# Splitting the norm before the first feed-forward: latents inside the projection, context inside the gated chunks

## The chip, the core and the metric

The kernel runs as one program on one core of a Trainium2 chip. The metric is the device time of one execution in microseconds (us), lower is better. Five engines work side by side, each on its own queue in the order in which its instructions stand: TensorE (PE, with its weight loads PEld), VectorE (DVE), ScalarE (ACT), GpSimd (POOL) and SyncE (SP, which issues the transfers). They wait for one another through semaphores.

## The reference, cut to what matters

Two transformer blocks of two layers each. The change lies in layer 0 of the first block, between the output projection of its mixer and its gated feed-forward. There are two token streams: 512 latents (`xl`) and 256 context tokens (`xc`), each of width 1024. Both take a residual, an RMS norm with modulation, and the feed-forward with a convolved gate of width 2816.

```python
def modulate(x, norm_w, shift, scale):
    return rms_norm(x, norm_w) * (1 + scale) + shift

def conv_ffn(h, w_up, conv_w, conv_b, w_down):
    up = h @ w_up
    gate, val = up[..., :D_FF], up[..., D_FF:]
    ...
    return (jax.nn.silu(gate_c) * val) @ w_down

    xl = xl + g1 * yl
    xl = xl + g2 * conv_ffn(modulate(xl, norm_ffn_w[l], sh2, sc2), ffn_w_up[l], ...)
    if with_ctx:
        xc = xc + cg1 * yc
        xc = xc + cg2 * conv_ffn(modulate(xc, norm_ffn_w[l], csh2, csc2), ffn_w_up[l], ...)
```

## The kernel before

Activations stand with features on the 128 partitions and tokens along the free axis, so width 1024 is eight tiles (`KT = 8`). Segment `s = 0` is the 512 latents, `s = 1` the 256 context tokens. A product in float32 is made of three rounded passes: a weight chunk is split into a high part (ACT, line 481, `split_hi`) and a low part (POOL, line 490, two halves, `split_lo`), the activation too, and PE adds high by high, low-activation by high and high by low weight (lines 888 to 890). Two slots hold weight chunks. The high part of chunk c+2 is written once PE has done with chunk c, and POOL and PE follow.

**The projection** (`wout0`, PE `project_both`) has eight chunks. Each is swept over the latents' eight tiles, then over the context's, and each sum goes to a PSUM bank of its own. DVE adds it to the residual X (line 3140), ACT squares it (590), DVE adds the squares up tile by tile in SA (601).

**The norm `n1`** has, for each segment, a mean on PE (line 637: the added squares and the last tile's square against a vector of ones), a root on ACT (660), a reciprocal on DVE (671, `invert`), and a spread on PE (683) that brings the factors back over the partitions into a bank. `means(pe, "n1")` does both means and then both spreads, behind the last chunk of the projection. Then each tile is made: DVE scales it out of the spread bank (691), ACT adds the shift into a high part (729) and, for odd tiles, writes the shifted whole (731), and the low part comes from DVE for even tiles (737) and from POOL for odd ones (744).

**The feed-forward** (`ffn`, stage `up0`) takes 44 weight chunks, four to a round: gate and value for two gated pairs, called c = 0 to 3 here. In the first round PE sweeps chunks 0 and 1 over the latents, then 0 and 1 over the context, and only chunk 0 waits for each tile of a segment (`h_there`). Chunk 2 follows, and from there the rest of `up0`. Before it makes the high part of chunk 2, ACT runs, in its own order, all shifts of both segments and then three Silu activations over condition vectors, which SP loads (line 1412, two into `arena` and one into the buffer of the squares, so only after the means have read it):

```python
                if l:
                    ...
                else:
                    late_silus((LATE_C, LATE_CC, LATE_C2), 3)
                with act.Fori(l, FT // 2 - 1) as i:
                    for c in range(2):
                        gate_pair(c, i)     # begins with split_hi(up, 2 * c + 2, 2 * i, (up, 2 * c, i))
```

POOL's order around the change is: low parts of chunks 0 and 1, odd tiles of the latents, odd tiles of the context, low parts of chunk 2 onward.

## Time and profile before

| what | value |
|---|---|
| time, median of 3 runs | 2271.38 us (2269.86 to 2274.02) |
| the profiled execution | 2269.67 us, of which its span is 2267.7 us |
| PE busy | 2211.0 us (98%), 13959 matmuls |
| DVE, ACT, POOL busy | 1177.3 (52%), 879.2 (39%), 932.8 us (41%) |
| granted PE clock, mean of the span | 0.995 |
| data moved | 245.40 MB, mean 108 GB/s |

Times in the views count from the start of the span. A bracket at a row's end is idle time just before the instruction, with what ended it. A row with "x3" stands for three instructions side by side, merged. The granted clock is 1.00 at 2.4 GHz and 0.50 at 1.2 GHz.

### The profile page before, as it was taken

The page shows a single profiled execution, that of the slowest core. Times are in us where ns is not written, and L with a number is a line of the kernel's source. Part 1 is how long each engine was busy: PE and PEld are TensorE (multiplying, and loading weights), DVE is VectorE, ACT ScalarE, POOL GpSimd, SP SyncE. Part 2 cuts the span into 40 slices and gives each one's busy share as a digit, 9 for nine tenths or more (in the row PEclk, how much of TensorE's full clock was granted, in tenths as well). Part 3 has the DMA queues.
Part 4 walks back from the last instruction along what each step waited for, and adds up shares of the span by engine and source line. Part 5 has one row for each costly group of instructions (what it writes and reads, how often), then busy time and mean ns, then how long its engine had stood idle before and what let it go on. Part 6 is the DMA issues. An engine that isn't in the chain of part 4 may idle for free.

```text
span 2267.7 us, 36911 instructions
## 1 busy us (share of the span) xinstructions
PE 2211.0 (98%) x13959; PEld 1900.5 (84%) x13959; DVE 1177.3 (52%) x1926; ACT 879.2 (39%) x1532; POOL 932.8 (41%) x767
## 2 busy tenths in 40 slices
PE   6999999999999999999999999999999999999998
PEld 4878979888888888889899988888888887788777
DVE  5785781657777763435244365553234115761273
ACT  5434353341111113325455442222444236742572
POOL 2435443343334443334353155555665441154323
PEclk9999999999999999999999999999999999999999
DMA  7242241125555541111211035553223332123212
GB/s 279 81 150 75 72 161 63 56 94 195 194 192 175 196 149 65 65 63 67 71 48 34 10 102 186 185 196 109 94 96 105 94 101 75 50 84 102 71 48 75
DMA packets 67720, 245.40 MB, mean 108 GB/s; under 512 B 7376, under 2 KB 11728, under 8 KB 66960
## 3 DMA queue, kind: packets, MB, share of 16 engines
q1 hardware_dynamic: 67360, 242.94, 31.3%
q8 instruction: 84, 1.38, 0.3%
q0 software_dynamic: 240, 0.79, 0.1%
q14 instruction: 36, 0.29, 0.0%
HBM read 240.81 MB, written 2.10 MB: 107 GB/s over the span
## 4 chain that ended last, share of the span: by engine, by line
PE 76%; issue 3%; DVE 2%; ACT 2%; POOL 1%; POOLq 0%; DVEq 0%; ACTq 0%
PE ps L888 14%; PE ps L889 14%; PE ps L890 14%; PE ps L1780 4%; PE ps L1783 4%; PE ps L1782 4%; PE ps L2010 2%; PE ps L1996 2%; PE ps L1948 1%; PE ps L925 1%; PE ps L926 1%; PE ps L927 1%; PE ps L637 1%; PE ps L2027 1%; POOL w_low L490 1%
## 5 line engine op out<-in xcount | busy, mean ns | idle before, releaser
L490 POOL TENSOR_TENSOR w_low<-ring,w_high 128x512 fp32r<-128x512 f32 (+2 forms) x534 | 746.0, 1418 | 1030.5 <-ACT w_high L481 1023.8
L481 ACT ACTIVATE w_high<-ring 128x1024 fp32r<-128x1024 f32 (+2 forms) x267 | 275.2, 1032 | 918.8 <-PE ps L890 623.7
L888 PE MATMUL ps<-h_high,w_high 128*128 128x512 f32 x1040 | 407.7, 392 | 4.4 <-DVE h_low L737 2.8
L889 PE MATMUL ps<-h_low,w_high 128*128 128x512 f32 x1040 | 405.9, 390 | 0.0
L890 PE MATMUL ps<-h_high,w_low 128*128 128x512 f32 x1040 | 405.4, 390 | 0.0
L888 PEld LDWEIGHTS ps<-h_high,w_high 128*128 128x128 f32 x1040 | 195.9, 188 | 47.9 <-issue 4.1
L890 PEld LDWEIGHTS ps<-h_high,w_low 128*128 128x128 f32 x1040 | 195.6, 188 | 41.4
L889 PEld LDWEIGHTS ps<-h_low,w_high 128*128 128x128 f32 x1040 | 195.9, 188 | 38.1
L3246 DVE TENSOR_TENSOR hidden<-arena,hidden 128x1536 fp32r<-128x1536 f32 (+1 forms) x42 | 87.2, 2076 | 193.3 <-ACT hidden L2363 193.3
L2913 DVE CUSTOM_DVE_ANT_0 const<-const,arena 128x1024 f32<-128x1024 f32 x96 | 154.9, 1629 | 56.5 <-DMA const<-late_w_dram 56.5
L1780 PE MATMUL ps<-hidden,w_high 128*128 128x512 f32 (+1 forms) x504 | 178.6, 354 | 0.0
L1782 PE MATMUL ps<-hidden,w_high 128*128 128x512 f32 (+1 forms) x504 | 178.5, 354 | 0.0
L1783 PE MATMUL ps<-hidden,w_low 128*128 128x512 f32 (+1 forms) x504 | 178.3, 354 | 0.0
L1783 PEld LDWEIGHTS ps<-hidden,w_low 128*128 128x128 f32 x504 | 95.2, 189 | 13.4
L890 PE MATMUL ps<-h_ctx_high,w_low 128*128 128x256 f32 x376 | 106.4, 283 | 0.0
L889 PE MATMUL ps<-h_ctx_low,w_high 128*128 128x256 f32 x376 | 106.4, 283 | 0.0
L1780 PEld LDWEIGHTS ps<-hidden,w_high 128*128 128x128 f32 x504 | 95.3, 189 | 13.2
L1782 PEld LDWEIGHTS ps<-hidden,w_high 128*128 128x128 f32 x504 | 95.3, 189 | 13.2
L888 PE MATMUL ps<-h_ctx_high,w_high 128*128 128x256 f32 x376 | 106.3, 283 | 0.0
L2592 ACT ACTIVATE arena<-arena 128x512 f32<-128x512 f32 (+2 forms) x128 | 81.0, 634 | 38.6 <-DVE arena L3430 38.3
L3169 DVE TENSOR_SCALAR arena<-ps,vecs 128x512 f32<-128x512 f32 x65 | 46.6, 717 | 65.9 <-PE ps L890 56.7
L889 PEld LDWEIGHTS ps<-h_ctx_low,w_high 128*128 128x128 f32 x376 | 72.0, 191 | 1.7
(553 smaller groups left out, 4747.8 us busy)
## 6 DMA issues: line engine op xcount, KB each, us to landing
const<-late_w_dram SPq DMA_DIRECT2D x112, 512.0 KB, 5.0
ring<-up_dram SPq DMA_DIRECT2D x88, 512.0 KB, 3.3
ring<-down_dram SPq DMA_DIRECT2D x44, 512.0 KB, 3.2
XB<-ada_dram SPq DMA_DIRECT2D x22, 768.0 KB, 5.4
ring<-winE_dram SPq DMA_DIRECT2D x32, 512.0 KB, 3.5
ring<-win_dram SPq DMA_DIRECT2D x20, 512.0 KB, 3.2
ring<-winC_dram SPq DMA_DIRECT2D x20, 512.0 KB, 3.5
arena<-ada_dram SPq DMA_DIRECT2D x10, 768.0 KB, 19.7
```

Source lines behind the costliest of these rows:

```text
L481: nc.scalar.activation(WH[p][:, 0:L], RAW[p][:, 0:L], ACT.Copy).then_inc(w_hi, 1)
L490: ins = nc.gpsimd.tensor_tensor(WL[p][:, to], RAW[p][:, to], WH[p][:, to].bitcast(F32), ALU.subtract)
L888: nc.tensor.matmul(bank[:, 0:n], wh[:, cols], hi, start=(k == 0), stop=False)
L889: nc.tensor.matmul(bank[:, 0:n], wh[:, cols], lo, start=False, stop=False)
L890: ins = nc.tensor.matmul(bank[:, 0:n], wl[:, cols], hi, start=False, stop=(k == kt - 1))
L1780: MM(to, wh[:, cols], hi, start=start and m % per == 0 and j == 0, stop=False, skip_group_check=True)
L1782: MM(to, wh[:, cols], lo, start=False, stop=False, skip_group_check=True)
L1783: ins = MM(to, wl[:, cols], hi, start=False, stop=stop and j == 1, skip_group_check=True)
L2592: A(at, at, ACT.Exp, scale=-1.0, bias=column(NM, kind, u, x), accum_out=column(LSUM, kind, u, x)).then_inc(e_p, 1)
L2913: nc.vector.tensor_tensor_reduce(LATE_W[t], LATE_W[t], vectors[x + t], 1.0, 0.0, ALU.mult, ALU.add, LATE_SUM[:, x + t:x + t + 1]).then_inc ...
L3169: TS(FA[:, c, a:a + n], bank[:, 0:n], cw[:, bass.ds(i * 2 + (FT + c), 1)], V(f"cb{l}")[:, bass.ds(i * 2 + c, 1)], ALU.mult, ALU.add).then_ ...
L3246: TT(lo, inner_pair(c, width, i), hi.bitcast(F32), ALU.subtract).then_inc(g_lo, 1)
```

## The change

The projection's last two chunks are swept in another order: chunk 6 latents, chunk 7 latents, chunk 6 context, then the mean of the latents, then chunk 7 context with the latents' spread inside it (before its last two tiles). `means(pe, "n1")` is gone. The context's mean stands inside chunk 0 of the feed-forward, in its sweep over the latents before tile 4, and the context's spread at the same place of chunk 1. ACT, DVE and POOL take their parts of the two segments in a matching order. The order of the squares in SA follows (`squared`). No arithmetic is added or left out.

```diff
             if stage in ADDED:
-                last = 2 if stage == "n6" else 0
+                last = 2 if stage in ("n1", "n6") else 0
...
                     for s in segs:
                         for c in range(2):
-                            split_features(pe, up, c, up, ns * c + s, KT, P, h_parts(norm), (s,),
-                                           ready=h_there(pe, norm) if c == 0 else None)
+                            def there(s, k):
+                                if c == 0:
+                                    h_there(pe, norm)(s, k)
+                                if s == 0 and k == KT // 2:
+                                    spread(pe, norm, 1) if c else mean(pe, norm, 1)
+
+                            split_features(pe, up, c, up, ns * c + s, KT, P, h_parts(norm), (s,), ready=there)
...
-                for c in range(2, KT):
+                for c in range(2, 6):
                     split_features(pe, "wout0", c, "wout0", 2 * c, KT, P, parted_, (0, 1))
+                for c, s in ((6, 0), (7, 0), (6, 1)):
+                    split_features(pe, "wout0", c, "wout0", 2 * c + s, KT, P, parted_, (s,))
+                mean(pe, "n1", 0)
+                (wh, wl), bank, order = await_parts(pe, "wout0", 7), open_bank(pe, "wout0", 15), (4, 5, 6, 7, 0, 1, 2, 3)
+                for k in order:
+                    if k == 2:
+                        spread(pe, "n1", 0)
...
             project_both()
-            means(pe, "n1")
             ffn(0, (0, 1), "n1", "n2")
...
-            out_squares("wout0", "n1", "up0", 2)
-            for s in range(2):
-                shift_high("n1", s)
...
+            for k in (6, 7):
+                await_taken(act, "wout0", 2 * k)
+                square("n1", 0, k)
+            root("n1", 0)
+            split_hi("up0", 0)
+            await_taken(act, "wout0", 13)
+            square("n1", 1, 6)
+            shift_high("n1", 0, range(3))
+            await_taken(act, "wout0", 15)
+            square("n1", 1, 7)
+            split_hi("up0", 1)
+            shift_high("n1", 0, range(3, 6))
+            root("n1", 1)
+            shift_high("n1", 0, range(6, KT))
+            shift_high("n1", 1)
...
+                    if stage == "up0":
+                        for j in (1, 3):
+                            odd_low("n1", 0, j)
                     split_lo(stage, 1)
...
-                        odd_lows(parted[stage], 0)
+                        odd_lows(parted[stage], 0, 5)
...
-            add_out("wout0", (0, 1), lambda k, s: mod[:, 0, 16 + k, s:s + 1], "n1")
             for s in range(2):
-                invert("n1", s)
-            for s in range(2):
-                scale_parted("n1", s)
+                add_square("n1", s, 5)
+            add_both(6, 0)
+            add_both(7, 0)
+            add_square("n1", 0, 6)
+            invert("n1", 0)
+            add_both(6, 1)
+            for j in range(KT + 2):
+                if j < KT:
+                    scale_tile("n1", 0, j)
+                if j >= 2 and j % 2 == 0:
+                    even_low("n1", 0, j - 2)
+                if j == 3:
+                    add_both(7, 1)
+                    add_square("n1", 1, 6)
+            invert("n1", 1)
+            scale_parted("n1", 1)
```

On PE, behind the last matmuls of the projection (`y_last`), the order before is both means (L637, the latents' with x3, then the context's), both spreads (L683), and the first tile of chunk 0:

```order
L890 MATMUL ps<-y_last,w_low 128x256
L637 MATMUL ps<-const,SA 128x1 [waits sq_used,bank_free0]
L637 MATMUL ps<-const,SA 128x1 x3
L637 MATMUL ps<-const,SQ 128x1 [waits sq_ready]
L637 MATMUL ps<-const,SQ 128x1 x3
L637 MATMUL ps<-const,SA 128x1 [waits sq_used,bank_free2]
L637 MATMUL ps<-const,SA 128x1
L637 MATMUL ps<-const,SQ 128x1 [waits sq_ready]
L637 MATMUL ps<-const,SQ 128x1
L683 MATMUL ps<-const,RS 128x128 [waits bank_free1,r_ready]
L683 MATMUL ps<-const,RS 128x128 x3
L683 MATMUL ps<-const,RS 128x128 [waits bank_free3,r_ready]
```

In the changed kernel the context's spread on PE stands in chunk 1 of the feed-forward, behind its fourth tile; the first row of that chunk also waits for bank 2, which ACT's root of the context frees. This is the fourth tile, the spread, and the fifth tile:

```order
L888 MATMUL ps<-h_high,w_high 128x512
L889 MATMUL ps<-h_low,w_high 128x512
L890 MATMUL ps<-h_high,w_low 128x512
L683 MATMUL ps<-const,RS 128x128 [waits bank_free3,r_ready]
L683 MATMUL ps<-const,RS 128x128
L888 MATMUL ps<-h_high,w_high 128x512
L889 MATMUL ps<-h_low,w_high 128x512
L890 MATMUL ps<-h_high,w_low 128x512
```

So what stood ahead of all of the feed-forward stands one and a half chunks into it. On ACT, the order before between the high part of chunk 1 (L481) and the latents' tiles is two roots, and then only shifts:

```order
L481 ACTIVATE w_high<-ring 128x1024 [waits bank_full7,raw_full1]
L660 ACTIVATE RS<-ps,small 128x4 [waits bank_full0,bank_full5]
L660 ACTIVATE RS<-ps,small 128x2 [waits bank_full2,bank_full5]
L729 ACTIVATE h_high<-arena,mod 128x512 [waits t_ready] x2
L731 ACTIVATE arena<-arena,mod 128x512
L729 ACTIVATE h_high<-arena,mod 128x512 [waits t_ready] x2
L731 ACTIVATE arena<-arena,mod 128x512
```

In the changed kernel ACT's queue, from the high part of chunk 0 on, is this (the two L590 rows are the context's last squares, the last row its root):

```order
L481 ACTIVATE w_high<-ring 128x1024 [waits bank_full5,raw_full0]
L590 ACTIVATE SQ<-XB 128x256 [waits sq_used,bank_free5]
L729 ACTIVATE h_high<-arena,mod 128x512 [waits t_ready] x2
L731 ACTIVATE arena<-arena,mod 128x512
L729 ACTIVATE h_high<-arena,mod 128x512 [waits t_ready]
L590 ACTIVATE SQ<-XB 128x256 [waits sq_used,bank_free7]
L481 ACTIVATE w_high<-ring 128x1024 [waits bank_full7,raw_full1]
L729 ACTIVATE h_high<-arena,mod 128x512 [waits t_ready]
L731 ACTIVATE arena<-arena,mod 128x512
L729 ACTIVATE h_high<-arena,mod 128x512 [waits t_ready] x2
L731 ACTIVATE arena<-arena,mod 128x512
L660 ACTIVATE RS<-ps,small 128x2 [waits bank_full2,bank_full5]
```

A square, chunk 1's high part and a root have moved in among the shifts of the latents. On POOL the order before is both chunks' low parts (L490, two rows each) and then all odd tiles (L744):

```order
L490 TENSOR_TENSOR w_low<-ring,w_high 128x512 [waits w_hi]
L490 TENSOR_TENSOR w_low<-ring,w_high 128x512
L490 TENSOR_TENSOR w_low<-ring,w_high 128x512 [waits w_hi]
L490 TENSOR_TENSOR w_low<-ring,w_high 128x512
L744 TENSOR_TENSOR h_low<-arena,h_high 128x512 [waits h_hi] x4
L744 TENSOR_TENSOR h_ctx_low<-arena,h_ctx_high 128x256 [waits h_hi] x4
```

In the changed kernel the same queue reads:

```order
L490 TENSOR_TENSOR w_low<-ring,w_high 128x512 [waits w_hi]
L490 TENSOR_TENSOR w_low<-ring,w_high 128x512
L744 TENSOR_TENSOR h_low<-arena,h_high 128x512 [waits h_hi] x2
L490 TENSOR_TENSOR w_low<-ring,w_high 128x512 [waits w_hi]
L490 TENSOR_TENSOR w_low<-ring,w_high 128x512
L744 TENSOR_TENSOR h_low<-arena,h_high 128x512 [waits h_hi] x2
L744 TENSOR_TENSOR h_ctx_low<-arena,h_ctx_high 128x256 [waits h_hi] x4
```

Chunk 1's low part stands between the latents' second and third odd tile.

## Rows read from the trace of the kernel before

**Rows 1.** Busy time by stretch of the span: end of the projection, the gap, the feed-forward.

```profile
484.80:491.60 6.80, 4.60 (x40) 4.33 (x38) 3.74 (x8) 3.90 (x8) 2.55 (x3) 0.79 0.15 44
491.60:495.50 3.90, 3.90 (x9) 2.91 (x10) 3.90 (x7) 3.84 (x7) 2.50 (x3) 0.50 0.91 347
...
sum 500.00, PE 499.12 PEld 441.92 DVE 312.28 ACT 117.51 POOL 181.82; mean PE 45.37 PEld 40.17 DVE 28.39 ACT 10.68 POOL 16.53
```

**Rows 2.** Timeline of PE, 476 to 512: start us, length us, engine, line, form, [idle <-releaser].

```profile
476.57 0.40 PE L888 MATMUL ps<-y_first,w_high 128*128 128x512 f32 x1
...
482.04 0.28 PE L888 MATMUL ps<-y_first,w_high 128*128 128x256 f32 x1
...
484.91 0.95 PE L637 MATMUL ps<-const,SA 128*128 128x1 f32 x8
...
487.51 1.85 PE L683 MATMUL ps<-const,RS 128*128 128x128 f32 x12
491.56 0.76 PE L888 MATMUL ps<-h_high,w_high 128*128 128x512 f32 x1 [2.20 <-DVE h_low L737]
...
498.83 0.50 PE L888 MATMUL ps<-h_high,w_high 128*128 128x512 f32 x1 [0.32 <-POOL h_low L744]
...
511.87 0.50 PE L888 MATMUL ps<-h_high,w_high 128*128 128x512 f32 x1 [0.88 <-POOL w_low L490]
```

**Rows 3.** Timeline of DVE, same stretch.

```profile
478.45 2.79 DVE L601 TENSOR_TENSOR SA<-SA,SQ 128x512 f32<-128x512 f32 x2 [1.19 <-ACT SQ L590]
482.24 0.75 DVE L3140 SCALAR_TENSOR_TENSOR XB<-ps,mod,XB 128x512 f32<-128x512 f32 x1 [1.00 <-PE ps L890]
...
488.69 2.06 DVE L691 SCALAR_TENSOR_TENSOR arena<-XB,gain,ps 128x512 f32<-128x512 f32 x3 [0.48 <-PE ps L683]
490.67 0.74 DVE L737 SCALAR_TENSOR_TENSOR h_low<-arena,mod,h_high 128x512 fp32r<-128x512 f32 x1
...
497.26 1.25 DVE L691 SCALAR_TENSOR_TENSOR arena<-XB,gain,ps 128x256 f32<-128x256 f32 x3
```

**Rows 4.** Timeline of ACT, same stretch.

```profile
485.63 0.42 ACT L590 ACTIVATE SQ<-XB 128x256 f32<-128x256 f32 x1 [1.98 <-DVE XB L3140]
485.96 1.04 ACT L481 ACTIVATE w_high<-ring 128x1024 fp32r<-128x1024 f32 x1
486.90 0.24 ACT L660 ACTIVATE RS<-ps,small 128x4 f32<-128x4 f32 x1
...
489.47 1.38 ACT L729 ACTIVATE h_high<-arena,mod 128x512 fp32r<-128x512 f32 x2 [1.46 <-DVE arena L691]
...
502.33 0.49 ACT L731 ACTIVATE arena<-arena,mod 128x256 f32<-128x256 f32 x1
502.84 1.28 ACT L2344 ACT_TABLE_LOAD   x1
...
508.15 1.06 ACT L481 ACTIVATE w_high<-ring 128x1024 fp32r<-128x1024 f32 x1 [1.06 <-PE ps L890]
```

**Rows 5.** Timeline of POOL, same stretch.

```profile
491.54 1.28 POOL L744 TENSOR_TENSOR h_low<-arena,h_high 128x512 fp32r<-128x512 f32 x1 [1.97 <-ACT arena L731]
...
497.48 1.29 POOL L744 TENSOR_TENSOR h_low<-arena,h_high 128x512 fp32r<-128x512 f32 x1 [0.69 <-ACT arena L731]
...
502.90 0.74 POOL L744 TENSOR_TENSOR h_ctx_low<-arena,h_ctx_high 128x256 fp32r<-128x256 f32 x1 [0.50 <-ACT arena L731]
509.29 2.53 POOL L490 TENSOR_TENSOR w_low<-ring,w_high 128x512 fp32r<-128x512 f32 x2 [5.65 <-ACT w_high L481]
```

**Rows 6.** The loads of the condition vectors (late_c), by their line.

```profile
L1412 SPq DMA_DIRECT2D SQ<-late_c_dram x1: 432/432/432, 490.4 to 490.4; - x1
...
DMA to landing us min/median/max: 4.5/5.3/6.9
```

**Rows 7.** PE near the start of the span: a wait, and the stretches behind it.

```profile
50.27 0.50 PE L1570 MATMUL ps<-in_parts_r,w_high 128*128 128x512 f32 x1 [2.05 <-POOL in_parts_q L744]
...
52.00:54.00 2.00, 2.00 (x11) 2.00 (x11) 1.85 (x5) 2.00 (x6) 1.39 (x2) 0.50 0.04 8
```

More of the change, by code:

```diff
@@ L1816, in project_both @@
                                 sums_done(ins, "wout0", 2 * c + s)
-                for c in range(2, KT):
+                for c in range(2, 6):
                     split_features(pe, "wout0", c, "wout0", 2 * c, KT, P, parted_, (0, 1))
+                for c, s in ((6, 0), (7, 0), (6, 1)):
[5 more added lines that the diff above has]
+                        spread(pe, "n1", 0)
+                    hi, lo = parted_(1, k)
+                    cols = slice(k * P, (k + 1) * P)
+                    MM, to = nc.tensor.matmul, bank[:, 0:CTX]
+                    MM(to, wh[:, cols], hi, start=(k == order[0]), stop=False)
+                    MM(to, wh[:, cols], lo, start=False, stop=False)
+                    ins = MM(to, wl[:, cols], hi, start=False, stop=(k == order[-1]))
+                sums_done(ins, "wout0", 15)
             project_both()
-            means(pe, "n1")
             ffn(0, (0, 1), "n1", "n2")
@@ L2421, in deferred_shift @@
                 shift_high(norm, 0, (KT - 1,))
-            out_squares("wout0", "n1", "up0", 2)
-            for s in range(2):
-                shift_high("n1", s)
+            load_table(ROOT)
+            for k in range(6):
+                split_hi("wout0", k + 2)
+                for s in range(2):
+                    await_taken(act, "wout0", 2 * k + s)
+                    square("n1", s, k)
+            for k in (6, 7):
[13 more added lines that the diff above has]
+            shift_high("n1", 1)
             ffn(0, (0, 1), "n2")
@@ L3280, in _, with add_both @@
             dve.wait_ge(x_in, 48)
-            add_out("wout0", (0, 1), lambda k, s: mod[:, 0, 16 + k, s:s + 1], "n1")
-            for s in range(2):
-                invert("n1", s)
-            for s in range(2):
-                scale_parted("n1", s)
+            def add_both(k, s):
+                bank, n = await_sums(dve, "wout0", 2 * k + s), SEGS[s][1]
+                taken(STT(X[s][:, k, :], bank[:, 0:n], mod[:, 0, 16 + k, s:s + 1], X[s][:, k, :], ALU.mult, ALU.add),
+                      "wout0", 2 * k + s)
+            for k in range(6):
+                for s in range(2):
+                    if k >= 2:
+                        add_square("n1", s, k - 1)
+                for s in range(2):
+                    add_both(k, s)
+            for s in range(2):
+                add_square("n1", s, 5)
[14 more added lines that the diff above has]
+            scale_parted("n1", 1)
             ffn(0, (0, 1), "n2")
```

## The prediction

> **What bounds the kernel now.** I read first the busy time by stretch. From 500 to 1000 us PE is busy 499.12 of 500 us [rows 1]: behind the start of the feed-forward nothing but PE's own work counts, so whatever moves the start of chunk 2 moves the end of the kernel by as much. The stretch that the change touches is the gap ahead of it. From 484.8 to 491.6 PE is called busy for 4.60 of 6.80 us, and the granted clock sinks; from 491.6 to 495.5 it is 0.50, and 9 matmuls take 3.9 us, 0.43 us each [rows 1].
>
> PE's own timeline shows what is in the gap. A latents' sweep of 24 matmuls runs from 476.57 to 482.04 (5.47 us, 0.23 each), a context's sweep on to 484.91 (2.87 us, 0.12 each). Then both means last until 487.51 (2.60 us for 24 short matmuls, so 1.73 latents and 0.87 context), the spreads follow, and PE waits 2.20 us for the first tile, at 491.56 [rows 2]. In that time DVE starts its first scale at 488.69, 1.18 us after the first spread began [rows 2, 3]. From first scale to first matmul it is 2.87 us.
>
> After that the tiles' makers set the pace and not PE. POOL begins its four odd tiles from 491.54 to 497.48, 1.98 us per pair of tiles [rows 5], while PE at full clock needs 6 x 0.23 = 1.37. So the half clock cost nothing there: PE still waited 0.32 us for the last odd tile at 498.83 [rows 2]. Last I followed what releases chunk 2 at 511.87, where PE waits 0.88 us for POOL's low part [rows 2]. ACT's last context shift ends at 502.82, the table load starts at 502.84, the three Silus end at 507.09 (the high part at 508.15 has 1.06 us idle before it, ended by PE) [rows 4], POOL's halves run from 509.29 to 511.82 [rows 5]. **ACT is thus only 1.06 us from being the one that releases chunk 2.** This small margin is what to watch.
>
> **What the change removes and gains.** In the new order the latents' sweep of chunk 6 starts at 476.57 - 8.34 = 468.23 (one chunk earlier), chunk 7's ends at 479.17, chunk 6's context at 482.04. The last latents' sum is added at once (0.75), squared (0.63 at 512 wide is bounded by the 0.42 for 256 below and the 0.75 of DVE above; I take 0.6) and tile 6 added up in half of 2.79 us [rows 3, 4]: all by about 481.6, so the mean at 482.04 does not wait. The cover is 0.4 us; beyond it each us counts in full. The mean takes 1.73, to 483.77; the root 0.24 [rows 4] and reciprocal end at about 484.4. PE goes on with 18 of the 24 context matmuls to 485.92, so the spread does not wait either. First scale 1.18 later, at 487.10, first matmul 2.87 later, at 489.97. PE has finished the projection at 487.8 and waits about 2.1 us. **The feed-forward starts 1.6 us earlier**, not 6: the wait for the first tile stays whole, and the mean and spread of the latents still take PE's time.
>
> **What it adds in chunk 0's sweep.** ACT starts shifting at 487.88 (0.78 behind the scale, as now: 488.69 to 489.47 [rows 3, 4]) and needs 0.66 per activation (1.98 for three). Tiles 0 to 2 are four of them, to 490.5. Then the context's last square, which waits for DVE's sum behind its fourth scale (487.10 + 2.06 + 0.74 for three scales and a low part [rows 3], about 0.6 and 0.4 for the fourth scale and the sum: 490.9), takes 0.42, and chunk 1's high part 1.04 [rows 4]. Only then, at 492.4, comes tile 3. Its odd shift ends at 493.75, POOL's low part (1.28) at 495.05. Without the two it would be 1.6 us earlier than now, at 493.2 (now 491.54 + 1.98 + 1.28 = 494.80 [rows 5]).
>
> POOL then makes chunk 1's low part, 2.53 us [rows 5], to 497.6, and only then tile 5, to 498.85. ACT meanwhile finishes tiles 4 and 5 at 495.6 and stands at the context's root, which waits for PE: tile 3 until 495.9, then the context's mean, 0.87, then the root, 0.25, to 497.1. Tiles 6 and 7 are three shifts, to 499.1, and the last low part ends at 500.4. PE's last tile, 0.69 us, ends at 501.2. Now it ends at 498.83 + 0.69 = 499.5. **The first sweep ends 1.7 us later although it starts 1.6 us earlier.**
>
> **What it makes late.** The context's spread stands behind four tiles of chunk 1: 501.2 + 12 x 0.23 = 504.0. The first context scale comes 0.7 later (half as many short matmuls as the latents'), at 504.7; it is now at 497.26 [rows 3]. From that scale to ACT's last context shift it is now 502.82 - 497.26 = 5.56 us [rows 3, 4], so it ends at 510.3. Behind it in ACT's queue come the table load and the Silus, 4.25 us (502.84 to 507.09), to 514.5, then chunk 2's high part and POOL's low part: from 508.15 to 511.87 it is 3.72 us [rows 2, 4]. **Chunk 2 starts at 518.2 instead of 511.87: 6.3 us later.** PE is not what holds it: its context tiles come until 504.7 + (502.90 + 0.74 - 497.26) = 511.1 [rows 3, 5], so chunk 0 ends at 511.4, chunk 1 at 514.3, and PE then waits 3.9 us. The 0.88 us wait has become the largest of the stretch.
>
> Costed at nothing: chunk 0's high and low part move from ACT's wait in the projection to 484.1 to 487.7, ahead of 489.97 by 2.2 us. SP's load of chunk 3 waits for POOL's low part of chunk 1, and the condition vectors stand behind it and behind the context's mean, so their issue goes from 490.4 to about 498; at the slowest landing of 6.9 us [rows 6] that is 505, and ACT wants them at 511.5. DVE's first gate work follows the Silus as it does now.
>
> **The clock.** The new 3.9 us wait stands between dense sweeps. Near the start of the span PE waits 2.05 us between matmuls of 512 columns, and in the stretch right behind, 52 to 54 us, the granted clock is 0.50 with PE busy 2.00 of 2.00 [rows 7]. So I expect a fall at chunk 2, where PE is the bound. As long a half-clock stretch as the one in the rows, 9 matmuls at 0.43 instead of 0.23 [rows 1, 2], costs 1.8 us; nothing is the lower bound, and a fall in the sparse first sweep that still lasts over the 12 matmuls ahead of the context's spread adds up to 12 x 0.20 = 2.4 above. I take 1.8, since the new wait is longer than the one that led to a fall. The Trainium skill (TensorE: Matmul & The Clock Gate, section A second HAM failure mode: psum-queue depth-cycling) says that a TensorE which idles briefly but often between groups of matmuls can swing between its clock levels and pay for each return. By that rule the broken first sweep would pay too, and the sum would be 8.7 to 12.3; the trace agrees so far as a fall stands behind that one short wait.
>
> **Sum.** 6.3 + 1.8 = 8.1 us later. The profiled execution took 2269.67 us, so 2277.8 by it; it stands 1.7 us under the median of 2271.38, by which it is 2279.5. I forecast 2279.
>
> **Rivals.** (1) *The clock falls twice*: half clock from the first sweep into chunk 1's first half, and again at chunk 2 over a stretch twice as long, 6.3 + 2.4 + 2 x 1.8 = 12.3, 2283.7. The rule of the Trainium skill above (TensorE: Matmul & The Clock Gate) would bring this about. For it: eight short waits in the first sweep; against: the sweep is dense at half clock, and the rows show that a dense stretch ends the fall. Chance 0.15.
> (2) *The insertions hide one another*: ACT and POOL fill their waits better than in my order of events, and the context's root finds its mean done. That is worth at most the 1.87 us that delay tile 3 (495.05 - 493.2) and some of the clock: 6.3 - 1.9 = 4.4, 2275.8 and below, within 0.2%. Chance 0.17.
> (3) *Not slower: the context's shifts run under PE's sweeps.* The place is the context's spread on PE. If it comes by 504.0 - 6.3 = 497.7, chunk 2 is no later than now. For that the first sweep has to end by 494.9, in 5.0 us, less than PE alone needs (5.47). If instead ACT's tail were not in the way, chunk 2 would come 1.6 us earlier at best, 2269.8: no change. Chance 0.07.
> (4) *It does all that a split norm can do*, and the whole of the gap goes: 511.87 - 484.91 = 26.96 us now, against 16.7 for four sweeps, 2.6 for means and 1.85 for spreads [rows 2], leaves 5.8 us, 2265.6, faster by 0.26%. Against it stand the 2.87 us that a first tile needs after its scale. Chance 0.05.
>
> **How the numbers follow.** The forecast, 6.3 with a clock loss between nothing and 4.2 us, has 0.56. A measurement of this kernel can tell about 0.2%, 4.5 us. Slower by more: 0.56 + 0.15 = 0.71; rivals 2 and 3 make 0.24 within it; faster 0.05. The range leaves out rival 4, rival 3 and the far end of rival 1, some 0.2 in all: from 2273, the middle of rival 2, to 2284.
>
> **What would show it.** Right: PE's first matmul of the feed-forward near 490; POOL's tile 5 behind chunk 1's low part; the context's scales starting near 504.7; ACT's table load near 510.3, with the next high part directly behind the Silus; and a PE wait of 3 to 4 us ended by POOL's w_low at chunk 2, near 518. Wrong: the context's scales before 500, or a chunk 2 that waits for less than 1 us.

## The result, and the profile after

| kernel | median of runs | profiled execution (span) |
|---|---|---|
| before | 2273.10 us (2268.61 to 2276.12, 11 runs) | 2269.67 (2267.7) |
| changed | 2280.61 us (2277.26 to 2283.83, 11 runs) | 2282.53 (2280.6) |

The changed kernel is slower by a little: its time is 1.0038 of that before, 95% interval 1.0030 to 1.0047. By 2271.38 that is 2280.0 us, against a forecast of 2279.0 and a range of 2273 to 2284.

The waits of PE between 480 and 900 us show at once where it stands (waited for: us in total, times, longest):

```profile
PE ps L888 <- POOL w_low L490: 3.5, 1, 3.5
PE ps L888 <- DVE h_low L737: 2.2, 1, 2.2
PE ps L888 <- POOL h_low L744: 0.8, 2, 0.4
```

The wait for the first tile (DVE's h_low) is as long as before [rows 2], and the wait for chunk 2's low part has grown from 0.88 to 3.47. The changed kernel's windows, to be read against rows 1:

```profile
484.80:491.60 6.80, 4.22 (x32) 3.56 (x30) 4.55 (x8) 4.03 (x8) 3.81 (x3) 0.98 0.22 77
491.60:495.50 3.90, 3.52 (x7) 1.94 (x8) 3.90 (x6) 3.90 (x7) 1.61 (x2) 0.50 0.00 0
495.50:500.00 4.50, 4.50 (x15) 3.87 (x16) 1.51 (x3) 1.68 (x5) 3.82 (x3) 0.50 0.20 66
...
520.00:525.00 5.00, 5.00 (x13) 3.90 (x12) 3.70 (x7) 1.79 (x2) 2.55 (x2) 0.50 0.74 230
...
530.00:1000.00 470.00, 470.00 (x2715) 416.15 (x2714) 295.80 (x410) 103.04 (x99) 173.88 (x114) 1.00 0.43 147
```

The half clock now spans most of the first sweep, and comes back at chunk 2 (520 to 525: 13 matmuls in 5 us, PE busy all the time). From 530 to 1000 us PE is busy 470.00 of 470.00 us, so nothing of a delay at chunk 2 is made good behind it.

PE's timeline: the latents' spread, the first matmul of the feed-forward, tile 3, the first matmul of chunk 1, the context's spread, the last matmul before the wait, chunk 2's latents, and its context:

```profile
486.32 1.05 PE L683 MATMUL ps<-const,RS 128*128 128x128 f32 x8
...
490.28 0.47 PE L888 MATMUL ps<-h_high,w_high 128*128 128x512 f32 x1 [2.20 <-DVE h_low L737]
...
495.23 0.79 PE L888 MATMUL ps<-h_high,w_high 128*128 128x512 f32 x1 [0.37 <-POOL h_low L744]
...
502.77 0.39 PE L888 MATMUL ps<-h_high,w_high 128*128 128x512 f32 x1
...
505.50 0.61 PE L683 MATMUL ps<-const,RS 128*128 128x128 f32 x4
...
515.69 0.28 PE L890 MATMUL ps<-h_ctx_high,w_low 128*128 128x256 f32 x1
519.43 0.80 PE L888 MATMUL ps<-h_high,w_high 128*128 128x512 f32 x1 [3.47 <-POOL w_low L490]
...
527.83 0.28 PE L888 MATMUL ps<-h_ctx_high,w_high 128*128 128x256 f32 x1
```

DVE, the first scale of the latents and of the context:

```profile
487.41 2.06 DVE L691 SCALAR_TENSOR_TENSOR arena<-XB,gain,ps 128x512 f32<-128x512 f32 x3 [2.25 <-PE ps L683]
...
506.15 1.26 DVE L691 SCALAR_TENSOR_TENSOR arena<-XB,gain,ps 128x256 f32<-128x256 f32 x3 [5.95 <-PE ps L683]
```

ACT, the two insertions, the context's root, its shifts, the table load, and the high part of chunk 2:

```profile
491.22 0.42 ACT L590 ACTIVATE SQ<-XB 128x256 f32<-128x256 f32 x1 [0.42 <-DVE XB L3323]
491.55 1.04 ACT L481 ACTIVATE w_high<-ring 128x1024 fp32r<-128x1024 f32 x1
...
498.47 0.26 ACT L660 ACTIVATE RS<-ps,small 128x2 f32<-128x2 f32 x1 [2.82 <-PE ps L637]
...
506.66 0.92 ACT L729 ACTIVATE h_ctx_high<-arena,mod 128x256 fp32r<-128x256 f32 x2 [6.10 <-DVE arena L691]
...
511.12 0.49 ACT L731 ACTIVATE arena<-arena,mod 128x256 f32<-128x256 f32 x1
511.63 1.28 ACT L2363 ACT_TABLE_LOAD   x1
...
515.78 1.04 ACT L481 ACTIVATE w_high<-ring 128x1024 fp32r<-128x1024 f32 x1
```

POOL, odd tiles 3 and 5 with chunk 1's low part between them, and chunk 2's low part:

```profile
493.89 1.28 POOL L744 TENSOR_TENSOR h_low<-arena,h_high 128x512 fp32r<-128x512 f32 x1 [2.34 <-ACT arena L731]
495.13 2.96 POOL L490 TENSOR_TENSOR w_low<-ring,w_high 128x512 fp32r<-128x512 f32 x2
498.05 1.27 POOL L744 TENSOR_TENSOR h_low<-arena,h_high 128x512 fp32r<-128x512 f32 x1
...
516.89 2.49 POOL L490 TENSOR_TENSOR w_low<-ring,w_high 128x512 fp32r<-128x512 f32 x2 [4.48 <-ACT w_high L481]
```

The chain is that of the prediction: a spread that comes 18 us behind the latents' first scale, ACT idle for 6.10 us before the context's shifts, then shifts, table load, Silus and high part without idle time, and PE waiting at the end.

**One measure for all kernels.** Times of single executions of one kernel differ by 5 to 12 us. Traces also differ in places far from the change: from 1150 to 1185 us, for example, among narrow matmuls, the mean granted clock is 0.95 in the profiled execution before and 0.85 in that of the changed kernel. So each trace is also read locally: from the first matmul of the projection's chunk 6 (latents) to the first of chunk 4 of the feed-forward. Chunk 4 follows chunk 3 without a wait.

| kernel | chunk 6 | chunk 2 | chunk 4 | stretch | ratio of times to before, 95% |
|---|---|---|---|---|---|
| before | 468.23 | 511.87 | 528.65 | 60.42 | 1 |
| changed | 468.60 | 519.43 | 539.05 | 70.45 | 1.0038, 1.0030 to 1.0047 |
| e1, spread early | 471.79 | 517.98 | 534.76 | 62.97 | 1.0005, 0.9995 to 1.0015 |
| e4, context alone | 471.62 | 523.12 | 542.42 | 70.80 | 1.0039, 1.0024 to 1.0054 |
| e2, weight before Silus | 471.57 | 520.62 | 539.98 | 68.41 | 1.0041, 1.0026 to 1.0055 |
| e5, wait filled | 468.20 | 519.10 | 535.93 | 67.73 | 1.0040, 1.0026 to 1.0054 |
| e7, queues | 474.66 | 524.28 | 543.88 | 69.22 | 1.0034, 1.0019 to 1.0048 |
| e8, spread and queues | 468.87 | 514.07 | 530.86 | 61.99 | 1.0004, 0.9994 to 1.0015 |
| e9, one copy | 468.49 | 512.97 | 529.75 | 61.26 | one run, 2271.33 us |
| e10, five copies | 474.77 | 522.52 | 541.39 | 66.62 | 1.0033, 1.0022 to 1.0044 |
| e11, weights ahead | 472.75 | 517.86 | 534.65 | 61.90 | 1.0004, 0.9993 to 1.0016 |

The changed kernel loses 10.03 us in this stretch, which is 0.44% and within the interval of its ratio. In every timed row the stretch's difference from 60.42, divided by 2272, lies in the interval beside it. The two profiled spans differ by 12.9; 0.37 of the rest lies ahead of chunk 6 and 2.5 behind it, where the clock from 1150 to 1185 us alone would make about 3.5 (an estimate, 35 us by 0.10). That clock is 0.95 in the traces of before, e1, e8, e9 and e11, and 0.80 to 0.90 in those of the six kernels that lose 6 us or more in the stretch. With one trace for each kernel it isn't shown whether the loss has this second part or chance put it there. The medians don't need it: they give the changed kernel a loss of 8.6 us by the ratio, less than its 10.03 in the stretch.

### The profile page after: what moved, and what is told of

Read it like the earlier page. It is cut to its first block, busy times and chain, and to the rows that moved or that the text cites. A ratio compares the mean times of both kernels' runs of the same rounds, so it can differ in the third digit from the quotient of the medians.

```text
span 2280.6 us, 36913 instructions
## 1 busy us (share of the span) xinstructions
PE 2220.6 (97%) x13959; PEld 1908.4 (84%) x13959; DVE 1172.8 (51%) x1926; ACT 879.1 (39%) x1532; POOL 935.2 (41%) x767
## 4 chain that ended last, share of the span: by engine, by line
PE 76%; issue 3%; ACT 2%; DVE 2%; POOL 1%; POOLq 0%; DVEq 0%; ACTq 0%
PE ps L888 14%; PE ps L889 14%; PE ps L890 14%; PE ps L1786 4%; PE ps L1788 4%; PE ps L1789 4%; PE ps L2029 2%; PE ps L2015 2%; PE ps L1967 1%; PE ps L925 1%; PE ps L926 1%; PE ps L927 1%; PE ps L637 1%; PE ps L2046 1%; POOL w_low L490 1%
## 5 line engine op out<-in xcount | busy, mean ns | idle before, releaser
L490 POOL TENSOR_TENSOR w_low<-ring,w_high 128x512 fp32r<-128x512 f32 (+2 forms) x534 | 747.4, 1421 | 1035.4 <-ACT w_high L481 1032.0
L481 ACT ACTIVATE w_high<-ring 128x1024 fp32r<-128x1024 f32 (+2 forms) x267 | 275.1, 1032 | 918.6 <-PE ps L890 622.8
L2953 DVE CUSTOM_DVE_ANT_0 const<-const,arena 128x1024 f32<-128x1024 f32 x96 | 147.7, 1551 | 55.0 <-DMA const<-late_w_dram 54.8
L888 PEld LDWEIGHTS ps<-h_ctx_high,w_high 128*128 128x128 f32 x376 | 72.0, 191 | 2.9 <-POOL h_ctx_low L744 1.2
```

The costliest lines, as they stand in the source:

```text
L481: nc.scalar.activation(WH[p][:, 0:L], RAW[p][:, 0:L], ACT.Copy).then_inc(w_hi, 1)
L490: ins = nc.gpsimd.tensor_tensor(WL[p][:, to], RAW[p][:, to], WH[p][:, to].bitcast(F32), ALU.subtract)
L888: nc.tensor.matmul(bank[:, 0:n], wh[:, cols], hi, start=(k == 0), stop=False)
L2953: nc.vector.tensor_tensor_reduce(LATE_W[t], LATE_W[t], vectors[x + t], 1.0, 0.0, ALU.mult, ALU.add, LATE_SUM[:, x + t:x + t + 1]).then_inc ...
```

## The experiments

The theory: the place of the context's spread makes ACT's tail late, and the tail makes chunk 2 late. The rival: the insertions in ACT's and POOL's queues, or the split of the norm itself, make the loss.

**e1: the context's spread one sweep earlier, all else as changed.**

```diff
-                                if s == 0 and k == KT // 2:
-                                    spread(pe, norm, 1) if c else mean(pe, norm, 1)
+                                if s == 0 and c == 0 and k == KT // 2:
+                                    mean(pe, norm, 1)
+                                if s == 0 and c == 0 and k == KT - 2:
+                                    spread(pe, norm, 1)
```

> Changed kernel with one edit: the context's spread moves from chunk 1 (before its fifth tile) into chunk 0's sweep over the latents, before its seventh tile; the mean stays. My theory (the late spread makes ACT's tail of context shifts and Silus late, and with it chunk 2's weights): the first context scale comes near 501.7 instead of 506.15, the Silus end near 511.4 instead of 515.9, PE and no longer ACT releases chunk 2's high part, and chunk 2 starts near 515.5 instead of 519.43 with a PE wait of about 0.9 instead of 3.47 us. Without the long wait the clock should not fall there, another 2.9 us. So 4 to 7 us less than the changed kernel, 1.5 to 4.5 us over the kernel before (ratio 1.0007 to 1.002). Rival (the insertions into ACT's and POOL's queues in the first sweep are the whole loss): nothing of the first sweep is changed, so within 1 us of the changed kernel, ratio near 1.0035.

Measured: 1.0005 (0.9995 to 1.0015), the stretch 62.97 us. PE's timeline of this kernel:

```profile
503.10 0.50 PE L888 MATMUL ps<-h_high,w_high 128*128 128x512 f32 x1 [2.13 <-POOL h_low L744]
...
503.90 0.61 PE L683 MATMUL ps<-const,RS 128*128 128x128 f32 x4
...
505.73 0.40 PE L888 MATMUL ps<-h_high,w_high 128*128 128x512 f32 x1
...
517.98 0.50 PE L888 MATMUL ps<-h_high,w_high 128*128 128x512 f32 x1 [0.87 <-POOL w_low L490]
...
523.55 0.28 PE L888 MATMUL ps<-h_ctx_high,w_high 128*128 128x256 f32 x1
```

The wait at chunk 2 is back at 0.87 us, and chunk 2's latents take 5.57 us as before. All insertions are still there: PE even waits 2.13 us for an odd tile. Of the 10.03 us, 7.48 went by moving one spread of four short matmuls, a little more than the 4 to 7 expected. The rival is refuted as the main cause. It does explain what is left: the row at 505.73 is the first of chunk 1, 33.94 us behind chunk 6. In the kernel before, PE's timeline has it here, 31.40 behind:

```profile
499.63 0.40 PE L888 MATMUL ps<-h_high,w_high 128*128 128x512 f32 x1
```

So PE's first sweep ends 2.54 us later, and chunk 2 comes 2.55 later.

**e4: the kernel before, with only the context's mean and spread deferred** (the projection's order, and the weights' places on ACT and POOL, stay; `there` is that of the change, and ACT and DVE take the context's steps in the matching order).

```diff
-            means(pe, "n1")
+            mean(pe, "n1", 0)
+            spread(pe, "n1", 0)
...
-                                           ready=h_there(pe, norm) if c == 0 else None)
+                                           ready=there)
...
-            for s in range(2):
-                shift_high("n1", s)
+            shift_high("n1", 0, range(6))
+            root("n1", 1)
+            shift_high("n1", 0, range(6, KT))
+            shift_high("n1", 1)
```

> Kernel before with only the context's part of the change: projection, squares and the latents' mean and spread as before, the context's mean in chunk 0 and its spread in chunk 1, its root behind tile 5 on ACT; chunk 1's weights are made ahead of the first tile as before. My theory: the deferral of the context costs everything; the first matmul comes near 491.4, ACT stands at the context's root, the context's spread is near 505, chunk 2 near 519 as in the changed kernel: ratio 1.003 to 1.0045. Rival (the insertion of chunk 1's weights between the latents' tiles is the loss): that insertion is absent here, so within 2 us of before, ratio 1.0000 to 1.001.

Measured: 1.0039 (1.0024 to 1.0054), stretch 70.80. PE's timeline here:

```profile
509.18 0.61 PE L683 MATMUL ps<-const,RS 128*128 128x128 f32 x4
...
523.12 0.80 PE L888 MATMUL ps<-h_high,w_high 128*128 128x512 f32 x1 [3.47 <-POOL w_low L490]
```

ACT's table load, ahead of the three Silus:

```profile
515.31 1.28 ACT L2351 ACT_TABLE_LOAD   x1
```

The same 3.47 us wait stands without any of the latents' part of the change. The deferral alone costs all of it, and the latents' earlier sums give back nothing that the times show.

**e10 and e9: the kernel before, with five copies, or one, ahead of the Silus on ACT.** The copies go over the condition vectors in place and change no value. Here nothing of the norm is touched; only ACT's tail grows.

```diff
                     act.wait_ge(late_c, 16 * loaded)
+                    for n in range(0 if l else 5):
+                        tail.link(A(vectors[n % 2], vectors[n % 2], ACT.Copy))
                     for x in vectors:
```

> The kernel before, with five such copies on ACT ahead of the three Silus, each waiting for the one before. Theory: 5.0 to 6.5 us of work less 1.06 of margin, so chunk 2 starts 4 to 5.4 us later behind a PE wait of 5 to 6.3 us that POOL's low part ends; the clock falls behind that wait, and the stretch from the start of chunk 6 of the projection to the start of chunk 4 of the feed-forward is 60.4 + 4 to 5.4 + 2 to 3 for the clock = 66.5 to 69 us; ratio to before 1.0025 to 1.004, though nothing of the norm is touched. Rival (the wait at chunk 2 is made good later, or the loss comes from the split norm itself): ratio within 1.001.

> The kernel before, with one more copy of 128 by 1024 values on ACT ahead of the three Silus, in place, and a wait for its end (it changes no value). It measures the margin of 1.06 us alone. Theory: the copy takes 1.0 to 1.3 us with its wait, ACT's idle time ahead of chunk 2's high part is used up, and chunk 2 moves by 0 to 0.3 us; PE's wait there stays 0.9 to 1.2 us. Rival (ACT's tail was already what releases chunk 2, or the margin is not a margin): chunk 2 moves by the whole copy, PE's wait there grows to 1.9 us or more.

ACT with five copies, from the context's last shift to the table load, and then PE, its first matmul of the feed-forward and chunk 2:

```profile
508.88 0.49 ACT L731 ACTIVATE arena<-arena,mod 128x256 f32<-128x256 f32 x1
509.28 1.05 ACT L2346 ACTIVATE arena<-arena 128x1024 f32<-128x1024 f32 x1
...
514.71 1.28 ACT L2348 ACT_TABLE_LOAD   x1
```

```profile
498.10 0.47 PE L888 MATMUL ps<-h_high,w_high 128*128 128x512 f32 x1 [2.46 <-DVE h_low L737]
...
522.52 0.80 PE L888 MATMUL ps<-h_high,w_high 128*128 128x512 f32 x1 [4.98 <-POOL w_low L490]
...
530.18 0.28 PE L888 MATMUL ps<-h_ctx_high,w_high 128*128 128x256 f32 x1
```

From first matmul to chunk 2 it is 24.42 us, against 20.31 before [rows 2]: 4.11 later. From first matmul to ACT's table load it is 16.61 us (514.71 - 498.10) against 11.28 (502.84 - 491.56) [rows 2, 4]: 5.33 later. So the margin is 1.22 us. The chunk's latents take 7.66 us instead of 5.57, and the ratio is 1.0033 (1.0022 to 1.0044). With one copy, PE's rows are

```profile
492.67 0.47 PE L888 MATMUL ps<-h_high,w_high 128*128 128x512 f32 x1 [2.06 <-DVE h_low L737]
...
512.97 0.50 PE L888 MATMUL ps<-h_high,w_high 128*128 128x512 f32 x1 [0.87 <-POOL w_low L490]
```

and the distance is 20.30, unchanged: one copy costs nothing. That execution's stretch is 0.84 longer for another reason, ahead of the copy: its spreads took 2.84 us instead of 1.85, so its first matmul came 24.18 us behind chunk 6 instead of 23.33. So a loss of the same kind, the wait and the half clock behind it, is had by a late tail on ACT alone, beyond a margin of about 1.2 us.

**e2: chunk 2's high part on ACT before the three Silus**, all else as changed.

```diff
                 else:
+                    split_hi(up, 2, 0, (up, 0, 0))
                     late_silus((LATE_C, LATE_CC, LATE_C2), 3)
+                    gate_pair(0, 0, False)
+                    split_hi(up, 3, 0, (up, 1, 0))
+                    split_hi(up, 4, 0, (up, 2, 0))
+                    gate_pair(1, 0, False)
+                    split_hi(up, 5, 0, (up, 3, 0))
-                with act.Fori(l, FT // 2 - 1) as i:
+                with act.Fori(1, FT // 2 - 1) as i:
```

> Changed kernel with ACT making chunk 2's high part before the three Silus and not behind them; the context's spread stays late. My theory (the Silus stand between the context's shifts and chunk 2's weights): PE ends chunk 0's context sweep near 512.8, the high part follows at once, chunk 2 starts near 516.6 instead of 519.43 with a wait of about 0.7 us, and the clock does not fall: 2.8 to 5.7 us less than the changed kernel, ratio to before 1.0013 to 1.0025. Rival (the context's tiles themselves are what PE is late by): no change, ratio near 1.0035.

Measured: 1.0041 (1.0026 to 1.0055), stretch 68.41: a miss. PE's timeline shows chunk 2, now early, and chunk 3:

```profile
520.62 0.50 PE L888 MATMUL ps<-h_high,w_high 128*128 128x512 f32 x1 [0.95 <-POOL w_low L490]
...
531.53 0.50 PE L888 MATMUL ps<-h_high,w_high 128*128 128x512 f32 x1 [2.29 <-POOL w_low L490]
```

DVE begins the gate's taps only at 522.73, behind ACT's Silus over the vectors; the gate's own Silu follows them on ACT at 526.94 and chunk 3's high part at 527.69. The wait has moved to chunk 3. The Silus have to be done ahead of the gate, so behind late shifts there is no place for them in ACT's queue that costs nothing. Ahead of the shifts, where ACT idles for 6.10 us in the changed kernel, no run put them; their vectors are issued there only from 498.55 to 499.43, and such loads took 4.4 us and more to land. A second part of the miss is no effect of the edit: the context's spread, ordered as in the changed kernel, came 37.64 us behind chunk 6 instead of 36.90; in this trace the granted clock was 0.63 from 502.8 to 507, behind a wait of 2.13 us in the first sweep.

**e5: the wait before chunk 2 filled with 15 matmuls whose sums nobody reads**, all else as changed.

```diff
+                if l == 0:
+                    warm = open_bank(pe, up, 6)
+                    for _ in range(15):
+                        nc.tensor.matmul(warm[:, 0:S], HH[0][:, 0, 0:P], HH[0][:, 0, :], start=True, stop=True)
                 for c in range(2, 4):
```

> Changed kernel with 15 extra matmuls of 512 columns (h_high by itself, into a bank that chunk 3 opens afterwards, result unused) between chunk 1's context sweep and chunk 2: 3.4 us of work in the 3.47 us in which PE waits. It prices the clock alone. My theory: chunk 2 starts at the same 519.4 or up to 0.3 later, the granted clock stays 1.00 and its latents' sweep takes 5.5 us instead of 8.4 (519.43 to 527.83): 2.5 to 3 us less than the changed kernel, ratio 1.0022 to 1.003. Rival (the fall is not due to the wait): the sweep stays slow, ratio 1.0035 to 1.004.

The window of 520 to 525 us in this kernel, for the row of the changed one above:

```profile
520.00:525.00 5.00, 5.00 (x25) 4.14 (x24) 3.71 (x8) 1.80 (x2) 2.71 (x2) 1.00 0.79 249
```

25 matmuls at full clock instead of 13 at half, and the stretch is 2.7 us shorter (67.73), with chunk 2 no earlier (50.90 us behind chunk 6, against 50.83). So in this trace what chunk 2 loses to the clock hangs on PE's idle time, not on the late weights as such. The ratio, 1.0040 (1.0026 to 1.0054), is not the 1.0022 to 1.003 expected but what the rival named. Its interval, from five runs, is 3 us wide to either side and can't tell 2.7 us from nothing, so by the times this run is inconclusive, and the clock's part rests on the trace.

**e7: another order on ACT and POOL**, PE's as changed. **e8: the same with e1's spread.**

```diff
-            split_hi("up0", 1)
             shift_high("n1", 0, range(3, 6))
-            root("n1", 1)
+            split_hi("up0", 1)
             shift_high("n1", 0, range(6, KT))
+            root("n1", 1)
...
-                        for j in (1, 3):
+                        for j in (1, 3, 5):
...
-                        odd_lows(parted[stage], 0, 5)
+                        odd_lows(parted[stage], 0, 7)
```

> The changed kernel, with another order of two queues: ACT makes the latents' tiles 0 to 5 before the high part of chunk 1, then tiles 6 and 7, and takes the context's root last; POOL makes the odd tiles 1, 3 and 5 before the low part of chunk 1. PE's order, and with it the context's spread in chunk 1, stays. Theory (the spread's place makes the loss): the first sweep ends 0.3 us (at half clock) to 1.9 us (at full clock) earlier, and chunk 2 with it, but chunk 2 still waits some 3 us for its low part: from the start of chunk 6 of the projection to the start of chunk 4 of the feed-forward 68.5 to 70.1 us, against 70.4 in the changed kernel and 60.4 before; ratio to before about 1.003. Rival (the insertions in ACT's and POOL's queues make the loss): that stretch falls to 65 us or less, ratio below 1.002.

> The changed kernel with the context's spread moved to chunk 0 behind tile 6, and with the other order of ACT's and POOL's queues as well (tiles 0 to 5 before chunk 1's parts, root last). Theory: with the tail of ACT out of the way the order of the queues decides the start of chunk 2 alone, so it gains the 0.3 to 1.9 us of the first sweep: from the start of chunk 6 of the projection to the start of chunk 4 of the feed-forward 61.1 to 62.7 us, against 63.0 with the spread alone moved and 60.4 before; ratio to before 1.000 to 1.001, so no gain over the kernel before. Rival (a split of the norm pays once both faults are mended): the stretch falls below 60 us, the 1.6 us of the earlier start come back, ratio 0.9995 or less.

Both came out as the theory said: stretches of 69.22 and 61.99 us. Chunk 2 in e7 by PE's timeline, and its table load by ACT's:

```profile
524.28 0.80 PE L888 MATMUL ps<-h_high,w_high 128*128 128x512 f32 x1 [3.47 <-POOL w_low L490]
```

```profile
516.47 1.28 ACT L2363 ACT_TABLE_LOAD   x1
```

PE's timeline in e8, the first matmul, tile 7 and chunk 2:

```profile
490.55 0.77 PE L888 MATMUL ps<-h_high,w_high 128*128 128x512 f32 x1 [2.20 <-DVE h_low L737]
...
501.02 0.50 PE L888 MATMUL ps<-h_high,w_high 128*128 128x512 f32 x1 [0.86 <-POOL h_low L744]
...
514.07 0.50 PE L888 MATMUL ps<-h_high,w_high 128*128 128x512 f32 x1 [0.88 <-POOL w_low L490]
```

The insertions are worth 1.2 us of the changed kernel's 10.03, if one trace of each can be set against the other: the first sweep of e2, ordered as in the changed kernel, ended 0.7 later than the changed kernel's. With both mended, e8 still isn't ahead of the kernel before: its first matmul comes 1.65 us earlier (21.68 behind chunk 6, against 491.56 - 468.23 = 23.33), but PE waits 0.86 us for tile 7 as late as 501.02, because POOL makes chunk 1's low part in front of it, and 0.80 us at 498.78 for the context's factors, which DVE inverts behind a low part.

**e11: e8 with both parts of chunk 1's weights ahead of all tiles.**

```diff
             square("n1", 1, 6)
+            split_hi("up0", 1)
             shift_high("n1", 0, range(3))
...
-            shift_high("n1", 0, range(3, 6))
-            split_hi("up0", 1)
-            shift_high("n1", 0, range(6, KT))
+            shift_high("n1", 0, range(3, KT))
...
-                    if stage == "up0":
-                        for j in (1, 3, 5):
-                            odd_low("n1", 0, j)
...
-                        odd_lows(parted[stage], 0, 7)
+                        odd_lows(parted[stage], 0)
```

> The changed kernel with the context's spread moved to chunk 0 behind tile 6, and with both parts of chunk 1's weights ahead of the latents' tiles: the high part on ACT behind the square of the context's tile 6, the low part on POOL ahead of all odd tiles, the context's root last. Theory: the slot for chunk 1 is free only when the projection ends, so the first shift and the first matmul come 0.5 to 0.9 us later than with the weights among the tiles, but no weight stands between the tiles any more, and the first sweep ends about 2.3 us earlier. From the start of chunk 6 of the projection to the start of chunk 4 of the feed-forward 59.6 to 60.5 us, against 62.0 with the weights among the tiles and 60.4 before; ratio to before 0.9996 to 1.0003, which the times cannot tell from 1. Rival (the split of the norm has another cost, on DVE or on PE): the stretch stays above 61.2 us.

Measured: 1.0004 (0.9993 to 1.0016), stretch 61.90, not the 59.6 to 60.5 expected. PE's timeline, the first matmul, tile 1, the context's mean, and the first matmul of chunk 1; then POOL's low part of tile 1:

```profile
495.42 0.77 PE L888 MATMUL ps<-h_high,w_high 128*128 128x512 f32 x1 [3.19 <-DVE h_low L737]
...
497.89 0.80 PE L888 MATMUL ps<-h_high,w_high 128*128 128x512 f32 x1 [0.84 <-POOL h_low L744]
...
501.51 0.50 PE L637 MATMUL ps<-const,SA 128*128 128x1 f32 x4
...
505.62 0.40 PE L888 MATMUL ps<-h_high,w_high 128*128 128x512 f32 x1
```

```profile
496.38 1.46 POOL L744 TENSOR_TENSOR h_low<-arena,h_high 128x512 fp32r<-128x512 f32 x1
```

The first matmul comes 22.67 us behind chunk 6, 0.99 later than in e8 (0.5 to 0.9 expected). PE then waits 0.84 us for tile 1, whose low part POOL begins only when it has made chunk 1's (493.46 to 496.41). From 497.89 on PE waits for nothing: it sweeps at half clock until about 501, and the context's mean (0.81 us) and spread (0.36) stand among its tiles. Chunk 1 begins 32.87 us behind chunk 6, 1.47 later than before, which is the whole of what the stretch loses (1.48). So the rival's number came out, and its reason in part: the context's mean and spread, which in the kernel before lay ahead of the first tile [rows 2], are PE's work inside the sweep.

**One count over all kernels.** Take ACT's table load, which starts the tail, as the time behind chunk 6: 34.61 us before (502.84 - 468.23), 43.03 in the changed kernel, 43.69 in e4, 41.81 in e7 and 39.94 in e10, so 8.42, 9.08, 7.20 and 5.33 later. Chunk 2 is 7.19, 7.86, 5.98 and 4.11 later: in all four, 1.22 or 1.23 less than the table load, whether the spread, the insertions or copies made it late. That is the margin. In e1, e8 and e11 the tail is less late, and chunk 2 is as late as the end of PE's own first sweep: by the start of chunk 1 2.54, 1.55 and 1.47 us, by that of chunk 2 2.55, 1.56 and 1.47.

## Why the prediction was right

**The mechanism and its place were right**, by e1, e4 and e10. Step by step, with the changed kernel's 0.37 us of earlier drift taken off:

- *Feed-forward 1.6 us earlier*: 1.65. The first matmul at 490.28 - 0.37 = 489.91, predicted 489.97; the wait of 2.20 us stayed whole.
- *First sweep ends at 501.2*: chunk 1 begins at 502.77 - 0.37 = 502.4. This step was 1.2 short. The order of events was as drawn up (square and high part among the shifts, chunk 1's low part between tiles 3 and 5, ACT at the root), but PE was priced at full clock. At half clock tile 3 took 1.44 us (495.23 to 496.67) instead of 0.69 and the context's mean 1.56 (to 498.23) instead of 0.87; ACT's root waits for that mean, and the last two tiles stand behind the root. The clock is about half of it: in e1 tile 3 and the mean ran at full clock, and the sweep, less the 0.36 us of the spread in it, still ended 33.58 us behind chunk 6 against 32.97 predicted, with PE waiting 2.13 us for POOL's tile 5. The bound of 2.4 us was named for the 12 matmuls behind the sweep, and those ran at full clock (502.77 to 505.50, 2.73 us).
- *Context's scale 0.7 behind its spread*: 0.65. *5.56 us to the end of the shifts*: 5.46 (506.15 to 511.61). *Table load and Silus 4.25*: 4.24. *3.72 from high part to chunk 2*: 3.65.
- *Chunk 2 later by 6.3*: 7.19 (50.83 behind chunk 6, against 43.64). The difference is the first sweep's 1.2, less 0.3 in the steps behind it.
- *PE waits 3.9*: 3.47, since its context sweeps ran later too.
- *Clock at chunk 2, 1.8*: 2.83 (519.43 to 527.83 is 8.40 us, before 5.57). The mechanism is shown by e5's trace; its size was taken from a half-clock stretch of 9 matmuls, and here it lasted over some 14.
- *Sum 8.1*: 10.03 in the stretch, and 7.5 by the medians (8.6 by the ratio, 6.8 to 10.7 by its interval). Two terms came out short by 0.9 and 1.0 us. That the forecast of 2279.0 lies 1 us from 2280.0 is therefore partly luck.

The rule of the Trainium skill (TensorE: Matmul & The Clock Gate, section A second HAM failure mode: psum-queue depth-cycling), by which the broken first sweep pays in clock as well, agrees with this trace as far as the granted clock is 0.50 from 491.6 to 500. The rows don't show that the breaks set it: e1, with the same breaks ahead of its tile 3, is back at full clock by 498.41, 4.9 us behind its first matmul, and stays there behind its wait of 2.13 us. The sum that it gave, 8.7 to 12.3, holds 10.03 where the plain sum stays below, but not by the term that it added, the 12 matmuls of chunk 1. Rival 1 was right that the half clock comes twice, wrong that it reaches into chunk 1, and too dear in size.

*The margin of 1.06 us* was the step that carried most, and e10 gives 1.2 for it; e9's one copy, which puts the table load 0.96 us later, stays inside it. Rival 2 (insertions hide one another) falls by the rows above: POOL ends tile 3 at 495.17 - 0.37 = 494.80, near the 495.05 of the order of events and not near 493.2, and ACT waits 2.82 us for the mean of the context's root. Rival 3 named the point from which it decides: a spread by 497.7. In e1 the spread comes at 503.90 - 3.56 = 500.34 on the clock of before, 2.64 too late, and chunk 2 is 517.98 - 3.56 - 511.87 = 2.55 too late. It agrees, but doesn't decide, since PE's own sweep ends as late there (2.54). Rival 4, the whole gap gained, has no run near it: e8 and e11, which undo the faults, stay 1.5 us behind the kernel before, since chunk 1's weights then stand ahead of a tile on POOL, and the context's mean and spread among the tiles on PE.

**What stays open.** Whether the split norm could gain at all with still another order isn't settled; the best of three (e1, e8, e11) is no different from before in its time. The clock's behaviour between 1150 and 1185 us wasn't studied.

## What to carry to other kernels

Before work is deferred on one engine, follow it to the next thing that some other engine's queue holds behind it: here four matmuls cost 0.36 us of PE, but ACT's shifts, three Silus and a weight split stood in line behind them, with 1.2 us to spare. Such a margin can be measured by itself with a few idle copies. And a wait on the bounding engine costs more than its length, since the dense work behind it can run at half clock: here 3.47 us of wait and 2.83 of clock.

## What the runs showed of the hardware

- The length of the half-clock stretch didn't follow the length of the wait: behind 3.47 us (changed, e7, e4) the way from chunk 2 to chunk 4 was 2.8, 2.8 and 2.5 us longer than the 16.78 of before, behind 4.98 us (e10) 2.1. Behind 0.87 us (e1, e9, e11) it was not longer at all, and behind 2.29 us (e2) the way from chunk 3 to chunk 4 was 8.45 us, before 8.34. Two waits of 2.13 us in the first sweep came out differently: behind that of e1 (503.10) the granted clock stayed 1.00, behind that of e2 (502.88) it was 0.63 from 502.8 to 507.
- Matmuls directly behind a wait can still run at full clock and then fall: in the changed kernel the first two went at 0.31 and 0.23 us from 490.28 on, and those from 492.20 on at 0.42 and more.
- VectorE's low part of a latents' tile took 1.26 us instead of 0.74 (494.45 in the changed kernel) where it overlapped POOL's odd low part of 493.89, and POOL's weight halves 2.96 instead of 2.52 where VectorE ran beside them. The Trainium skill (SBUF — State Buffer, section SBUF: two separate sides) says that the two share one pair of ports, and that an operation of either can hold it whole and block the other; these rows agree in direction. In the changed kernel PE waited for neither of the two; in e11 the first matmul did wait for such a low part (494.03, 1.25 us).
